# Output stores from another queue, and projections that wait for their operands half by half

## The chip, the cores and the metric

The kernel runs on one core of a Trainium2 chip. The metric is the time of one execution on the device in microseconds; of several runs the median is given. The core has five engines that run on their own and meet at semaphores: TensorE (PE in the profile, PEld for its weight loads), VectorE (DVE), ScalarE (ACT), GpSimd (POOL) and SyncE (SP). DMAs are issued from SP, ACT and POOL. Those of SP and ACT show in the profile as the hardware queues, those of POOL as the software queue.

## What is computed

One inference step of an encoder for 256 prompt tokens and 64 sample tokens (320 in all), model width 1024, two layers. Cut to what matters:

```
for i in range(2):
    up, us = rmsnorm(xp, g_mix[i]), rmsnorm(xs, g_mix[i])
    yp, ys = mlstm(up, us) if i == 0 else pool_mix(up, us)       # layer 0 / layer 1
    xp, xs = xp + yp, xs + ys
    kp, vp = rmsnorm(mem, g_mem[i]) @ w_k, rmsnorm(mem, g_mem[i]) @ w_v
    xp = xp + cross_attend(rmsnorm(xp, g_xattn[i]), kp, vp, w_q, w_o)
    xs = xs + cross_attend(rmsnorm(xs, g_xattn[i]), cache_k[i], cache_v[i], w_q, w_o)
    xp = xp + peer(rmsnorm(xp, g_ffn[i]), w_peer_q, peer_keys, expert_u, expert_v)
    xs = xs + peer(rmsnorm(xs, g_ffn[i]), ...)
y_prompt, y_sample = rmsnorm(xp, g_final), rmsnorm(xs, g_final)  # and all the carried states
```

All is in fp32. The products with the weights are made of three products of rounded halves: of the weight and of the activation a high part (fp32r) and a low part (the rest) are formed, and hi·hi, hi·lo and lo·hi are summed.

## The kernel before

It is written engine by engine by hand: each engine has one program, in which the order of the code is the order of execution, and semaphores hold the engines together. Nothing is scheduled.

**Tiles.** The 320 tokens are three tiles of 128, 128 and 64 rows (`TILES`). To use a normalised tile `u` as an operand, PE turns it: `transposes` (L800) makes two jobs per tile, each of four 128-column blocks, so three tiles give six jobs in the order tile 0 first half, tile 0 second half, tile 1 first half and so on. For each job ACT copies the high part out of PSUM (`copy_transposes`, L1194) and DVE subtracts to get the low part (`empty_transposes`, L1569), and then adds one to `d_emptied`. Job n of the D banks is thus done when `d_emptied` is n + 1. `DJ[stage]` is the number of a stage's first job; the four D banks are used in turn, and `d_bank(n)` makes PE wait until job n − 4 is emptied. The first half of a tile holds the rows k = 0 to 3 of the eight 128-deep slices (k) over which a product with a weight is summed, the second half k = 4 to 7.

**Weights** come by 2 MB chunks from SP (L510). ACT rounds a chunk's quarters (L1232 in the projections, L1366 in the PEER stage), adding to `w_hi_ready`, POOL (in some stages DVE) forms the rest (L467, L700), adding to `w_lo_ready`. Both write a ring that holds four quarters.

**Products** on PE have two forms. `split_block` (L804, matmuls L815 to L817) has the weights stationary and takes a quarter q (two slices k) at a time, 24 matmuls for one block of 128 features; `feature_major` (stages qk and xq) and the PEER query (pq) use it. `token_major` (L831, matmuls L844, L847, L852) has the tokens stationary and goes through k = 0 to 7, for each k over all the tiles, five hi and three lo matmuls of 512 columns where there are three tiles, four and two where there are two; two calls make the 1024 columns. Stages v, o, out, memk, memv and xo use it.

**The stages with the changed waits**, in the order of the program: the first norm's transposes, then qk (once); the mLSTM output's transposes (yT), eight state products (L963), then out (once); and for each of the two layers memT then memk (the memory's keys), xn then the turned memory keys (memkT, L984) then xq, the attention (`av`) then xo, and fn then pq. Before each of those products PE waits once for the whole set of transposed halves, `d_emptied` at the stage's last job. In the attention, `av_order` makes 16 jobs per layer: for each head two transposes of probabilities and two feature jobs (L1019), and DVE writes each feature job out as one slice k of the next product's operand, in four operations (L1815 to L1818). The last head's two features are the jobs 14 and 15.

**The end.** After the last PEER stage DVE finishes `x` (L2072), ACT takes the row statistics (L1180, L1181), DVE normalises the tiles in the order samples, prompt 0, prompt 1 (L1562, adding to `u_ready`), and POOL stores each as it is ready (L761), then waits for all stores (L762 to L765). POOL's work before that is the gathering of expert rows (L729). Line L242, named in the profile for the end of each engine's program, is where the block of the five programs is closed: each engine runs a DRAIN there and they meet at a barrier.

## Time and profile before

| | us |
|---|---|
| median of 3 runs | 2447.32 |
| lowest, highest | 2447.02, 2448.24 |
| the profiled execution's own time | 2450.18 |
| its span, first to last instruction | 2448.4 |
| PE busy | 2360.5 |
| PE's weight loads busy | 2095.0 |
| DVE, ACT, POOL busy | 1496.3, 1280.1, 1458.7 |
| mean granted TensorE clock | 0.988 |

A stretch of work is named by its start in the span. The setup and mLSTM stages are at 0 to 245 us, layer 0's memory, attention and projections at 245 to 400, its PEER stage at 400 to 1330, and the same of layer 1 up to 2430, with the output at the very end. Where idle time of an engine is shown in square brackets, the name behind the arrow is the operation that ended it. Names of engines with a q (POOLq, PEldq) are their instruction queues, for instructions that do no work on data. The share of busy time tells little here, since PE is at 96% nearly throughout; what matters is what PE waits for at a stage's start, and what stands behind the last matmul.

### The profile page before, as it was taken

To read this page: it belongs to the slowest core of one execution; us is meant where nothing else is said; L and a number is where in the kernel's file an instruction comes from. 1 tells how busy PE (TensorE), PEld (TensorE's weight loads), DVE (VectorE), ACT (ScalarE), POOL (GpSimd) and SP (SyncE) were. 2 spreads that over 40 slices of the span, in tenths; PEclk is the share of its full clock that TensorE was granted. 3 is DMA by queue.
4 is the path that set the end of the run, shared out by engine and by line. 5 is a ranking of instruction groups with operands and counts; after the bars stand their busy time and mean duration, and the time that the engine had idled before them with its cause. 6 is when DMAs were issued, how large, how long until landed. Compare 5 with 4: busy or idle time off the path is not lost.

```text
span 2448.4 us, 43649 instructions
## 1 busy us (share of the span) xinstructions
PE 2360.5 (96%) x13862; PEld 2095.0 (86%) x13862; DVE 1496.3 (61%) x3045; ACT 1280.1 (52%) x2864; POOL 1458.7 (60%) x1803
## 2 busy tenths in 40 slices
PE   7999999999999999999999999999999999999997
PEld 7766877998999999888887877998999999888885
DVE  3244444897755332788886444897665332788885
ACT  4334544455765555545454544455775555545453
POOL 6634436689668888773210436688668888773210
PEclk9998999999999999999999999999999999999998
DMA  5324433244788886899986333243688886899983
GB/s 204 130 86 133 160 138 121 104 148 144 230 294 269 272 262 226 318 344 330 358 321 254 138 138 112 97 155 128 226 296 282 259 270 227 313 349 326 358 317 125
DMA packets 219860, 548.60 MB, mean 224 GB/s; under 512 B 49569, under 2 KB 135585, under 8 KB 194414
## 3 DMA queue, kind: packets, MB, share of 16 engines
q1 hardware_dynamic: 135422, 402.62, 47.6%
q0 software_dynamic: 31536, 117.53, 13.0%
q10 hardware_dynamic: 52800, 27.27, 3.9%
q8 instruction: 42, 0.69, 0.1%
q14 instruction: 60, 0.49, 0.1%
HBM read 478.81 MB, written 68.55 MB: 224 GB/s over the span
## 4 chain that ended last, share of the span: by engine, by line
PE 65%; DVE 12%; POOL 12%; issue 8%; ACT 2%; DMA 1%; POOLq 0%; SPq 0%; ACTq 0%; DVEq 0%
PE psum L1046 28%; POOL w_split L700 12%; PE psum L815 7%; PE psum L817 6%; PE psum L816 6%; PE psum L847 6%; PE psum L852 3%; PE psum L1103 2%; DVE arena L1870 1%; DVE arena L1908 1%; PE psum L1068 1%; PE psum L1001 1%; DVE arena L1910 1%; PE psum L1019 1%; DVE arena L1840 1%
## 5 line engine op out<-in xcount | busy, mean ns | idle before, releaser
L700 POOL TENSOR_TENSOR w_split<-w_ring,w_split 128x256 fp32r<-128x256 f32 x1152 | 890.5, 789 | 235.0 <-ACT w_split L1366 179.6
L815 PE MATMUL psum<-uT_split,w_split 128*128 128x320 f32 x2560 | 813.9, 318 | 20.9 <-POOL w_split L700 10.9
L817 PE MATMUL psum<-uT_split,w_split 128*128 128x320 f32 x2560 | 793.8, 310 | 0.0
L816 PE MATMUL psum<-uT_split,w_split 128*128 128x320 f32 x2560 | 793.6, 310 | 0.0
L1366 ACT ACTIVATE w_split<-w_ring 128x256 fp32r<-128x256 f32 x1152 | 473.3, 418 | 465.6 <-PE psum L817 439.4
L815 PEld LDWEIGHTS psum<-uT_split,w_split 128*128 128x128 f32 x2560 | 483.6, 189 | 41.1 <-POOL w_split L700 25.3
L1046 PE MATMUL psum<-v_hl,p_hl 128*128 128x512 f32 x2064 | 483.2, 389 | 1.9 <-DVE p_hl L2021 1.9
L816 PEld LDWEIGHTS psum<-uT_split,w_split 128*128 128x128 f32 x2560 | 484.0, 189 | 0.0
L817 PEld LDWEIGHTS psum<-uT_split,w_split 128*128 128x128 f32 x2560 | 483.1, 189 | 0.0
L1046 PEld LDWEIGHTS psum<-v_hl,p_hl 128*128 128x128 f32 x2064 | 386.8, 188 | 84.9 <-DVE p_hl L2021 3.1
L2015 DVE TENSOR_TENSOR arena<-arena 128x256 f32<-128x256 f32 x256 | 176.8, 728 | 334.5 <-ACT arena L1495 291.5
L467 POOL TENSOR_TENSOR w_split<-w_ring,w_split 128x256 fp32r<-128x256 f32 x328 | 240.2, 748 | 118.8 <-ACT w_split L1232 106.1
L1478 ACT ACTIVATE v_hl<-w_ring 128x1024 fp32r<-128x1024 f32 x172 | 182.3, 1060 | 228.8 <-PE psum L1046 198.6
L1232 ACT ACTIVATE w_split<-w_ring 128x256 fp32r (+1 forms) x416 | 157.8, 413 | 242.6 <-PE psum L852 171.9
L2026 DVE TENSOR_TENSOR v_hl<-w_ring,v_hl 128x1024 fp32r<-128x1024 f32 x172 | 211.6, 1230 | 101.2 <-ACT v_hl L1478 89.9
L1046 PE MATMUL psum<-uT_split 128*128 128x512 f32 x1008 | 242.1, 389 | 0.0
L1046 PEld LDWEIGHTS psum<-uT_split 128*128 128x128 f32 x1008 | 189.2, 188 | 39.3
L735 POOL DMA_INDIRECT cst<-acts,cst x128 | 141.7, 1107 | 39.0 <-issue 39.0
L729 POOL DMA_INDIRECT w_ring<-peer_v,cst x64 | 80.9, 1264 | 115.9 <-DVE psum L1948 102.3
L1478 ACT ACTIVATE uT_split<-w_ring 128x1024 fp32r<-128x1024 f32 x84 | 89.0, 1060 | 111.3 <-PE psum L1046 98.1
L729 POOL DMA_INDIRECT arena<-peer_v,cst x64 | 68.4, 1069 | 114.7 <-DVE psum L1948 106.8
L2026 DVE TENSOR_TENSOR uT_split<-w_ring,uT_split 128x1024 fp32r<-128x1024 f32 x84 | 103.0, 1227 | 46.5 <-ACT uT_split L1478 46.4
(294 smaller groups left out, 2597.8 us busy)
## 6 DMA issues: line engine op xcount, KB each, us to landing
w_ring<-peer_u SPq DMA_DIRECT2D x128, 1024.0 KB, 5.1
w_ring<-peer_v SPq DMA_DIRECT2D x256, 512.0 KB, 5.5
arena<-gates SPq DMA_DIRECT2D x32, 1024.0 KB, 8.1
gates<-w_ring POOLq DMA_DIRECT2D x22, 1024.0 KB, 7.2
weighed<-arena ACTq DMA_DIRECT2D x36, 512.0 KB, 6.7
arena<-weighed SPq DMA_DIRECT2D x36, 512.0 KB, 7.1
w_ring<-w_pq SPq DMA_DIRECT2D x8, 2048.0 KB, 8.1
gates<-arena POOLq DMA_DIRECT2D x10, 1024.0 KB, 8.7
```

The costliest lines, as they stand in the source:

```text
L467: eng.tensor_tensor(dst, raw, chunk_quarter(name, local, i, q, 0)[1].bitcast(F32), ALU.subtract).then_inc(w_lo_ready, 1)
L700: pool.tensor_tensor(split_pair(q, 1), quarter(raw, m, q), split_pair(q, 0).bitcast(F32), ALU.subtract).then_inc(w_lo_ready, 1)
L729: pool.indirect_dma_start(out=row_slot[k % SLOTS], out_offset=None, in_=t_in["peer_v"].rearrange("l b p k d -> (l b p k) d"), in_offset=ba ...
L815: pe.matmul(bank[:, 0:TOK], hi, uT_hi[:, k, :], start=k == 0, stop=False)
L816: pe.matmul(bank[:, 0:TOK], hi, uT_lo[:, k, :], start=False, stop=False)
L817: last = pe.matmul(bank[:, 0:TOK], lo, uT_hi[:, k, :], start=False, stop=k == KD - 1)
L1046: last = pe.matmul(psum[:, 2 + 2 * t + n, :], lhs, vh[:, part, n * 512:(n + 1) * 512], start=False, stop=False, skip_group_check=True)
L1232: act.activation(dst, raw, ACT.Copy).then_inc(w_hi_ready, 1)
L1366: act.activation(split_pair(q, 0), quarter(raw, m, q), ACT.Copy).then_inc(w_hi_ready, 1)
L1478: act.activation(vhl[b % 3][:, 0, :], v_raw[b % 4], ACT.Copy).then_inc(vhi_ready, 1)
L2015: return dve.tensor_tensor(halves_of, halves_of, g_blocks[buffer][:, :, r // 2, :, r % 2], ALU.mult)
L2026: dve.tensor_tensor(vhl[b % 3][:, 1, :], v_raw[b % 4], vhl[b % 3][:, 0, :].bitcast(F32), ALU.subtract).then_inc(v_split, 1)
```

## The change

Two things are changed. The three output stores and the final waits for all stores stand at the end of SP's program and no longer at the end of POOL's. And where PE waited for all jobs of a transposed set, it waits for one more than the first halves' last job but one before the slices k = 0 to 3, that is for the last tile's first half, and for the last tile's second half before k = 4 (before the quarters 0 and 2 of the first block in `split_block`, before every k in `token_major`). Before the attention's output projection it waits at each k for the job that made this feature.

```diff
@@ sync, at its end
+            for place, t in enumerate(ORDER["final"]):
+                off, rows = TILES[t]
+                sp.wait_ge(u_ready, 18 + place + 1)
+                dst = t_out["y_p"][off:off + rows] if t < 2 else t_out["y_s"]
+                sp.dma_start(dst, u[0:rows, t, :]).then_inc(y_stored, 16)
+            sp.wait_ge(mem_stored, 64)
+            sp.wait_ge(pool_stored, 32)
+            sp.wait_ge(state_stored, 64)
+            sp.wait_ge(y_stored, 48)
@@ gpsimd, at its end
-            for place, t in enumerate(ORDER["final"]):
-                off, rows = TILES[t]
-                pool.wait_ge(u_ready, 18 + place + 1)
-                dst = t_out["y_p"][off:off + rows] if t < 2 else t_out["y_s"]
-                pool.dma_start(dst, u[0:rows, t, :]).then_inc(y_stored, 16)
-            pool.wait_ge(y_stored, 48)
-            pool.wait_ge(mem_stored, 64)
-            pool.wait_ge(pool_stored, 32)
-            pool.wait_ge(state_stored, 64)
@@ tensor: split_block
+            def split_block(i, per, base, bank, filled=a_filled, quarters=range(4), turned_tiles=None):
                 for q in quarters:
+                    if turned_tiles is not None and q % 2 == 0:
+                        pe.wait_ge(d_emptied, DJ[turned_tiles] + 5 + q // 2)
                     pe.wait_ge(w_lo_ready, at(i, 4 * per, base + q + 1))
@@ tensor: token_major
+                            parts=(uT_hi, uT_lo), k_ready=None):
                 for k in range(KD):
                     ...
+                    if k_ready is not None:
+                        pe.wait_ge(d_emptied, k_ready(k))
                     pe.wait_ge(w_hi_ready, ready)
@@ tensor: the stages
-            pe.wait_ge(d_emptied, DJ["mixn0"] + 6)
-            feature_major("qk", 4)
+            feature_major("qk", 4, "mixn0")
...
-            pe.wait_ge(d_emptied, DJ["yT"] + 6)
-                token_major("out", "out", c, TILES, base=3 * c)
+                token_major("out", "out", c, TILES, base=3 * c, k_ready=lambda k: DJ["yT"] + 5 + k // 4)
...
-                pe.wait_ge(d_emptied, DJ[f"memT{l}"] + 4)
-                    token_major(f"memk{l}", f"memk{l}", c, mt, base=2 * c, parts=(mT_hi, mT_lo))
+                    token_major(f"memk{l}", f"memk{l}", c, mt, base=2 * c, parts=(mT_hi, mT_lo),
+                                k_ready=lambda k: DJ[f"memT{l}"] + 3 + k // 4)
...
-                pe.wait_ge(d_emptied, DJ[f"xn{l}"] + 6)
-                feature_major(f"xq{l}", 2)
+                feature_major(f"xq{l}", 2, f"xn{l}")
...
-                pe.wait_ge(d_emptied, DJ[f"av{l}"] + 16)
+                features = {2 * h + k - 2: n for n, h, k in av_order(l) if k >= 2}
-                    token_major(f"xo{l}", f"xo{l}", c, TILES, base=3 * c)
+                    token_major(f"xo{l}", f"xo{l}", c, TILES, base=3 * c, k_ready=lambda k: features[k] + 1)
...
-                pe.wait_ge(d_emptied, DJ[f"fn{l}"] + 6)
-                            split_block(i, 8, split_base(l, m), a_bank(AJ[f"pq{l}"] + m, i, 8))
+                            split_block(i, 8, split_base(l, m), a_bank(AJ[f"pq{l}"] + m, i, 8),
+                                        turned_tiles=f"fn{l}" if m == 0 else None)
```

On PE, at the start of layer 0's output projection xo, behind the last feature job (`arena` holds the values, `uT_split` and `p_hl` the attention's features for prompt and samples, `w_split` the split weights). Before:

```order
L847 MATMUL psum<-w_split,uT_split 128x512 [waits d_emptied,w_hi_ready]
L847 MATMUL psum<-w_split,uT_split 128x512
L847 MATMUL psum<-w_split,uT_split 128x512 [waits d_emptied]
L847 MATMUL psum<-w_split,uT_split 128x512
L844 MATMUL psum<-w_split,p_hl 128x512 [waits d_emptied]
L852 MATMUL psum<-w_split,uT_split 128x512 [waits w_lo_ready]
L852 MATMUL psum<-w_split,uT_split 128x512
L852 MATMUL psum<-w_split,p_hl 64x512
L847 MATMUL psum<-w_split,uT_split 128x512 [waits w_hi_ready]
```

And now, with the first row of the next slice as the last:

```order
L854 MATMUL psum<-w_split,uT_split 128x512 [waits d_emptied,w_hi_ready]
L854 MATMUL psum<-w_split,uT_split 128x512
L854 MATMUL psum<-w_split,uT_split 128x512 [waits d_emptied]
L854 MATMUL psum<-w_split,uT_split 128x512
L851 MATMUL psum<-w_split,p_hl 128x512 [waits d_emptied]
L859 MATMUL psum<-w_split,uT_split 128x512 [waits w_lo_ready]
L859 MATMUL psum<-w_split,uT_split 128x512
L859 MATMUL psum<-w_split,p_hl 64x512
L854 MATMUL psum<-w_split,uT_split 128x512 [waits w_hi_ready,d_emptied]
```

No instruction moved. The first wait on `d_emptied` is for another number, the waits of the three banks (one per tile) are as they were, and each later slice has a wait on `d_emptied` beside the one on `w_hi_ready`.

At the end of POOL's program before:

```order
L729 DMA arena<-peer_v,cst 128x1024 [waits rows_used] x4
L761 DMA y_s<-arena 64x1024 [waits u_ready]
L761 DMA y_p<-arena 128x1024 [waits u_ready] x2
L242 UNCONDITIONAL_BRANCH [waits pool_stored,state_stored,mem_stored,y_stored]
```

And at the end of SP's program now, behind the last expert rows that SP loads:

```order
L569 DMA w_ring<-peer_v 128x1024 [waits v_split] x11
L625 DMA y_s<-arena 64x1024 [waits u_ready]
L625 DMA y_p<-arena 128x1024 [waits u_ready] x2
L242 UNCONDITIONAL_BRANCH [waits state_stored,y_stored,pool_stored,mem_stored]
```

The stores and the four waits moved as they are; POOL's program now goes from its last gather to the end of the block.

## Rows read from the trace of the kernel before

**Rows 1.** The page: shares of the chain of work that ended last.

```profile
PE 65%; DVE 12%; POOL 12%; issue 8%; ACT 2%; DMA 1%; POOLq 0%; SPq 0%; ACTq 0%; DVEq 0%
```

**Rows 2.** Line L242: engine, operation, count, ns min/median/max, first to last start (us).

```profile
L242 POOLq EVENT_SEMAPHORE  x2: 17/17/17, 2448.2 to 2448.3; - x2
L242 SPq DRAIN  x1: 123/123/123, 2414.8 to 2414.8; - x1
...
L242 POOLq DRAIN  x1: 9136/9136/9136, 2439.0 to 2439.0; - x1
```

**Rows 3.** Line L2188, the barrier at the kernel's start, same columns.

```profile
L2188 POOLq DRAIN  x1: 183/183/183, 0.3 to 0.3; - x1
```

**Rows 4.** Timeline of the end: start, us, engine, line, operation [idle before <-releaser].

```profile
2356.71 0.94 POOL L729 DMA_INDIRECT arena<-peer_v,cst  x1 [4.56 <-DVE psum L1948]
...
2434.21 1.28 DVE L1562 SCALAR_TENSOR_TENSOR arena<-x_sb,small,gain_rows 128x1024 f32<-128x1024 f32 x1
...
2435.80 0.54 POOL L761 DMA_DIRECT2D y_p<-arena  x1 [0.81 <-DVE arena L1562]
```

**Rows 5.** DMA issues of 2436 to 2449: queue, count, KB each, us to landing.

```profile
y_p<-arena POOLq DMA_DIRECT2D x1, 512.0 KB, 3.0
```

**Rows 6.** DMA issues of 2414 to 2422, same columns.

```profile
w_ring<-peer_v SPq DMA_DIRECT2D x1, 512.0 KB, 3.2
```

**Rows 7.** Timeline of 2411 to 2416: the wait that this SP load follows.

```profile
2413.19 1.23 DVE L2026 TENSOR_TENSOR v_hl<-w_ring,v_hl 128x1024 fp32r<-128x1024 f32 x1 [3.29 <-ACT v_hl L1478]
...
2414.44 0.33 SPq L569 DMA_DIRECT2D w_ring<-peer_v  x1
```

**Rows 8.** Waits of PE's matmuls: us in total, times, longest.

```profile
PE psum L847 <- DVE v_hl L1569: 4.3, 2, 2.5
...
PE psum L815 <- DVE uT_split L1569: 2.8, 2, 1.4
PE psum L847 <- DVE p_hl L1818: 2.5, 2, 1.2
```

**Rows 9.** Timeline of layer 0's memory keys, 247 to 250.

```profile
247.24 2.48 DVE L1569 TENSOR_TENSOR v_hl<-psum,v_hl 128x512 fp32r<-128x512 f32 x4
...
249.78 0.50 PE L847 MATMUL psum<-w_split,v_hl 128*128 128x512 f32 x1 [1.86 <-DVE v_hl L1569]
```

**Rows 10.** Timeline of the attention's end, layer 0, 354 to 362.

```profile
353.82 3.61 PE L1019 MATMUL psum<-arena 128*128 128x256 f32 x22
...
357.09 0.21 DVE L1818 TENSOR_TENSOR p_hl<-psum,p_hl 128x64 fp32r<-128x64 f32 x1
...
358.66 1.19 PE L847 MATMUL psum<-w_split,uT_split 128*128 128x512 f32 x4 [1.24 <-DVE p_hl L1818]
```

**Rows 11.** Timeline of fn and the first query block, layer 0, 395 to 400.

```profile
394.93 3.14 DVE L1569 TENSOR_TENSOR uT_split<-psum,uT_split 128x512 fp32r<-128x512 f32 x6
...
395.75 2.78 POOL L700 TENSOR_TENSOR w_split<-w_ring,w_split 128x256 fp32r<-128x256 f32 x4
...
398.13 0.42 PE L815 MATMUL psum<-uT_split,w_split 128*128 128x320 f32 x1 [1.40 <-DVE uT_split L1569]
```

**Rows 12.** Timeline of the first projection, 14 to 20.

```profile
16.66 0.63 PE L815 MATMUL psum<-uT_split,w_split 128*128 128x320 f32 x1 [1.77 <-POOL w_split L467]
```

**Rows 13.** The last chain before stage out: start us, us, what.

```profile
205.56 7.13 PE psum L963 x16
```

**Rows 14.** Timeline of 275 to 280: the turned memory keys, between xn and xq.

```profile
277.10 2.04 PE L984 MATMUL psum<-cst,arena 128*128 128x128 f32 x16 [0.23 <-DVE uT_split L1569]
```

**Rows 15.** PE's own waiting instructions at L779 (bank waits in the PEER stages).

```profile
L779 PEldq EVENT_SEMAPHORE  x32: 51/51/51, 404.8 to 1571.8; - x32
```

**Rows 16.** PE in xo's first chunk, 358 to 373: busy us, mean ns, idle before.

```profile
L847 PE MATMUL psum<-w_split,uT_split 128*128 128x512 f32 x32 | 8.8, 395 | 1.2 <-DVE p_hl L1818 1.2
...
L847 PEld LDWEIGHTS psum<-w_split,uT_split 128*128 128x128 f32 x32 | 5.9, 188 | 3.0 <-DVE p_hl L1818 1.4
```

**Rows 17.** Busy by stretch: length, PE, PEld, DVE, ACT, POOL, PEclk, DMA share, GB/s.

```profile
399.00:402.40 3.40, 3.40 (x15) 3.40 (x15) 0.00 (x0) 0.83 (x2) 1.47 (x2) 0.50 0.00 0
```

More of the change, by code:

```diff
@@ L805, in u_transposes @@
                 transposes(stage, lambda t, rows, b: u[0:rows, t, b * P:(b + 1) * P], TILES, 3 * norm, u_ready)
-            def split_block(i, per, base, bank, filled=a_filled, quarters=range(4)):
+            def split_block(i, per, base, bank, filled=a_filled, quarters=range(4), turned_tiles=None):
                 for q in quarters:
+                    if turned_tiles is not None and q % 2 == 0:
+                        pe.wait_ge(d_emptied, DJ[turned_tiles] + 5 + q // 2)
                     pe.wait_ge(w_lo_ready, at(i, 4 * per, base + q + 1))
@@ L818, in split_block, with feature_major @@
                     last.then_inc(quarter_used if q < 3 else filled, 1)
-            def feature_major(name, n_chunks):
+            def feature_major(name, n_chunks, turned_tiles):
                 def pair(i):
                     for m in range(8):
-                        split_block(i, 8, SPLIT[name, 0][0] + 4 * m, d_bank(DJ[name] + m, i, 8), d_filled)
+                        split_block(i, 8, SPLIT[name, 0][0] + 4 * m, d_bank(DJ[name] + m, i, 8), d_filled,
+                                    turned_tiles=turned_tiles if m == 0 else None)
                 if n_chunks == 2:
@@ L831, in token_major @@
             def token_major(stage, name, local, tiles, bank_of=d_bank, filled=d_filled, jobs=DJ, base=0, folded=True,
-                            parts=(uT_hi, uT_lo)):
+                            parts=(uT_hi, uT_lo), k_ready=None):
                 banks = [None] * len(tiles)
```

## The prediction, made before the changed kernel ran

> **What bounds the kernel now.** I read the page's shares of the last chain first [rows 1]. PE has 65% of it, and DVE and POOL have 12% each, which they spend in the PEER stages that the change leaves alone. So time can be won only where PE stands idle at the start of a product, or behind the last matmul. For the first I read the waits of PE's matmuls by line [rows 8], and for each place the timeline. The reader should see which operation ended the wait, since that is what a finer wait can pass. For the second I read the timeline of the end and the instructions of line L242, where the profile shows each engine's DRAIN.
>
> **The end.** DVE finishes the last tile at 2434.21 + 1.28 = 2435.49, POOL starts the store 0.31 us later at 2435.80 [rows 4], and the store lands 3.0 us after that, at 2438.8 [rows 5]. No engine has work left, yet the span ends at 2448.4. Between stands one row: a DRAIN on POOL's queue from 2439.0 with 9136 ns, and the barrier's last semaphores at 2448.2 to 2448.3, 17 ns each [rows 2]. The DRAIN begins after POOL has waited for the stores, so it lies wholly on the path. SP's DRAIN took 123 ns, right behind a load that SP had just issued [rows 2].
>
> With the change POOL has nothing left after its last gather at 2356.71 + 0.94 = 2357.65 [rows 4]. If its DRAIN takes the same 9.1 us there, it ends near 2366.8, with 70 us to spare before the last store. The end is then SP's. SP started a load 0.02 us after the DVE operation that it waited for (2413.19 + 1.23 = 2414.42, start 2414.44) [rows 7], and that load, of the same 512 KB and with no other transfer about, took 3.2 us from issue to landing [rows 6]. So the store goes out at 2435.51 and lands at 2438.7. Then I put 0.15 us to the DRAIN (POOL's stood some 0.2 us behind its landing), 0.12 us for SP's DRAIN, and 0.25 us for the barrier (from POOL's end, 2439.0 + 9.14 = 2448.15, to 2448.4) [rows 2]. This makes 2439.2, which is **9.2 us** less. The store itself gains 0.1 us of that, the rest is the DRAIN. The store is a write where the row is a read; a write that took a microsecond more would take that off.
>
> The Trainium skill, page "DMA: Bandwidth & Descriptors", section "Specifications", puts the first byte of a DMA from SP or ACT at about 0.6 us and of one from GpSimd at about 1 us. By that the store would land 0.4 us sooner than by the rows, and the sum would be 0.4 us better. The two rows of equal size show 3.2 us from SP and 3.0 us from POOL from issue to landing, so the trace doesn't bear this out, and I go by the rows.
>
> **The projections**, in the order of the program.
>
> *qk* (once). PE's first matmul at 16.66 was released by POOL's split of the weights, not by the transposes [rows 12]. Nothing is gained.
>
> *out* (once). Between the yT jobs and out stand eight state products, and the bank waits of the last need the yT jobs emptied already. In the chain PE runs through them for 7.13 us and then goes on [rows 13]. Nothing is gained. *xq* (twice) is the same case: the fourth group of turned memory keys needs a bank that is free only when job 6 of xn is emptied, so the wait is before those transposes [rows 14] and not before xq. Nothing.
>
> *memk* (twice). Four half tiles, which DVE empties in 2.48 us, 0.62 us apart (247.24 to 249.72), and PE starts at 249.78 [rows 9]. Rows k = 0 to 3 need the first three. PE starts 0.62 us sooner, and what it finds next is there: the fourth is emptied 0.62 us later, while PE needs over 3 us for four slices. The stage then runs as a ring of PE, ACT and DVE at one pace, so its end moves with its start. 2 x 0.62 = **1.2 us**.
>
> *xo* (twice). PE ends the attention's products at 353.82 + 3.61 = 357.43 and starts xo at 358.66, when DVE has written the last feature [rows 10]. That feature is needed at k = 7 only. What is late next? The bank of the third tile needs job 14 emptied, which is at 357.09 + 0.21 = 357.30 [rows 10], so it is free when PE comes. The two idle times are 2.5 us in sum [rows 8], and all of it goes: **2.5 us**. Slice k = 7 comes some 12 us later and doesn't wait.
>
> *pq* (twice). DVE empties six halves in 3.14 us; the last two, of the 64-row tile, are 0.33 us apart, which is what is left of 3.14 us after four of 0.62 us, halved. PE starts at 398.13, right behind the last, and POOL's first quarter has been split since 395.75 + 0.7 [rows 11]. Quarter 0 needs the fifth half only. Idle 2.8 us in two [rows 8], of which 2 x 0.33 = **0.7 us** goes. Between nothing and the whole 2.8 us I take this, since the fifth half is the last that quarter 0 needs.
>
> *The waits added.* Five single waits go, and eight come in each of ten calls of `token_major`, some 80. Behind each stands all of PE's work, and ACT, which refills the weights' ring when PE has used them. PE's instruction for a further wait takes 51 ns [rows 15]. If each were exposed, this is 80 x 0.051 = 4.1 us. But in xo's first chunk, where slice 0 already carries the waits for three banks beside those for the weights, the 32 matmuls of L847 have 1.2 us of idle before them in all, and that is the wait at the start [rows 16]. So satisfied waits pass while PE works on what is queued, and I take 0, with 4.1 us as the upper bound. Below nothing it can't go, since a wait makes nothing faster.
>
> *The clock.* After a sparse stretch of PE the granted clock stood at 0.50 from 399.0 to 402.4, the lower level of 1.2 GHz [rows 17], in the middle of the first query blocks. Such a stretch costs up to half its length, 1.7 us, and one lies near four of the six starts that move. A start that moves by 0.3 to 1.3 us can lose such a stretch or meet one. I take no change, and up to three either way, 5 us, as the outer bound.
>
> **The sum.** 9.2 + 1.2 + 2.5 + 0.7 = 13.6 us. The stages behind hang on these by semaphores and carry their transfers along, so a start that is earlier stays so. The profiled execution took 2450.18 us with a span of 2448.4, and would take 2436.6. The median of the runs shown is 2447.32, so I predict 2447.32 - 13.6 = **2433.7 us**.
>
> **The rivals.**
> *The DRAIN is longer under the profiler.* The profiled execution is 2.9 us over the median. If all of that is in the DRAIN, the true one takes 6.3 us and the gain is 2.9 us less: 2436.6 us. Nothing else in the profile speaks for it.
> *The last 9 us stay.* The DRAIN might be long because it comes at the very end, whoever waits there, or POOL's might wait for the others. Then the change doesn't do what it says at the end and only the projections' 4.4 us are left: 2442.9 us. For this speaks that at the kernel's start POOL's took 183 ns [rows 3], so its length is no constant. Against it: the DRAINs of the other engines end before, and SP's took 0.12 us in the midst of its load [rows 2].
> The Trainium skill, page "VectorE: DVE Perf Modes", section "The DRAIN you can't avoid", has the DRAINs at a program's start and end at about 12 ns, the same on all five engines. By that rule there is no long DRAIN to hide and this rival would be the forecast, 2442.9 us; the row of 9136 ns speaks against the rule here.
> *The waits are exposed.* 4.1 us at 51 ns each: 2437.8 us.
> *Slower.* A wait at each k could keep PE from loading the next weights ahead. Then each of the 80 costs a weight load of 188 ns [rows 16] and its own 51 ns, 19.1 us together, and the time is 2433.7 + 19.1 = 2452.8 us. It decides from 0.23 us a wait, (13.6 + 4.9) / 80. Against it stands that the weights' waits at each k of today don't do this [rows 16].
> *The starts don't pay*, because a transfer or another engine is late next by as much: 2447.32 - 9.2 = 2438.1 us. Against it: SP issues each of these loads when a chunk two before has been used, so they move with the stages.
>
> **How the numbers follow.** The forecast 0.75; the profiler's share 0.07; the last 9 us stay 0.05; waits exposed 0.05; starts don't pay 0.04; slower 0.02; something else that is faster 0.02. A measurement of this kernel can tell some 0.2% (4.9 us) from no change: faster is below 2442.4, slower above 2452.2. Faster sums to 0.93, the same 0.05, slower 0.02. The range takes in the exposed waits and the starts that don't pay, and for the clock two stretches less on the lower side: 2430.3 to 2438.3.
>
> **What would show it.** In the changed kernel's trace POOL's DRAIN should stand near 2357 to 2367 less the few us of the projections, with 9 us, and the span should end under 0.6 us behind the last landing. PE's idle before L847 of xo should be gone, that before memk 0.6 us shorter and before pq 0.3 us shorter; before qk, out and xq nothing should change. The slices k = 1 to 7 should stand as close as now. The prediction is wrong if POOL's DRAIN moves with the end, if SP's store takes well over 3.2 us, or if idle time of PE grows inside the chunks.

## The result, and the profile of the changed kernel

The changed kernel took 2438.02 us in the median of four executions (2437.41 to 2443.15). The kernel before, timed beside it, took 2447.78 us in the median of four (2447.02 to 2455.87). The ratio is 0.9955 with a 95% interval of 0.9944 to 0.9967. So the change makes the kernel faster, by 9.8 us by the medians and by about 11 us (8 to 14) by the ratio. 13.6 us were forecast, and 2433.7 us as the time. The range of 2430.3 to 2438.3 us holds it, near its upper end.

The profiled execution took 2443.15 us with a span of 2441.3 us, the longest of the four. Its span is 7.1 us shorter than that of before, 2448.4 us. So two things are to be found: what the change won, and what kept 3 to 4 us in the executions together, and 6.5 us in this profile, from being won.

The shares of the last chain, from the page. The row answers to [rows 1].

```profile
PE 63%; POOL 13%; DVE 12%; issue 9%; ACT 2%; DMA 1%; POOLq 0%; SPq 0%; ACTq 0%; DVEq 0%
```

**The end.** The instructions of line L242 (engine, operation, count, ns min/median/max, first to last start), beside [rows 2]:

```profile
L242 POOLq DRAIN  x1: 11644/11644/11644, 2359.1 to 2359.1; - x1
...
L242 SPq COMPARE_BRANCH  x1: 41/41/41, 2440.9 to 2440.9; - x1
L242 SPq DRAIN  x1: 7/7/7, 2441.1 to 2441.1; - x1
L242 SPq EVENT_SEMAPHORE  x1: 17/17/17, 2441.3 to 2441.3; - x1
```

The timeline of the end (start, us, engine, line, operation), beside [rows 4]:

```profile
2436.79 1.74 SPq L625 DMA_DIRECT2D y_p<-arena  x2
2436.88 1.29 DVE L1566 SCALAR_TENSOR_TENSOR arena<-x_sb,small,gain_rows 128x1024 f32<-128x1024 f32 x1
```

The two stores of y_p among the DMA issues (KB each, us from issue to landing), beside [rows 5]:

```profile
y_p<-arena SPq DMA_DIRECT2D x2, 512.0 KB, 2.7
```

POOL's DRAIN now starts at 2359.1, and POOL takes up its last gather 0.2 us later:

```profile
2359.30 0.94 POOL L739 DMA_INDIRECT arena<-peer_v,cst  x1 [4.49 <-DVE psum L1952]
```

The DRAIN takes 11.6 us and ends near 2371, 67 us before the last store. DVE ends its last operation at 2436.88 + 1.29 = 2438.17, the store lands 2.7 us after its issue, and SP's DRAIN takes 7 ns. From the end of DVE's last operation to the end of the span it is 3.1 us. Before it was 2448.4 - 2435.49 = 12.9 us [rows 2, 4]. The end gained 9.8 us, of which 9.2 were forecast.

**The starts.** The first is the timeline of layer 0's memory keys, beside [rows 9].

```profile
247.59 2.48 DVE L1573 TENSOR_TENSOR v_hl<-psum,v_hl 128x512 fp32r<-128x512 f32 x4
...
249.54 0.73 PE L854 MATMUL psum<-w_split,v_hl 128*128 128x512 f32 x2 [1.26 <-DVE v_hl L1573]
```

The next is the timeline of the attention's end in layer 0, beside [rows 10].

```profile
351.74 5.45 PE L1023 MATMUL psum<-arena 128*128 128x256 f32 x32
...
357.00 1.17 PE L854 MATMUL psum<-w_split,uT_split 128*128 128x512 f32 x4
...
358.15 0.21 DVE L1822 TENSOR_TENSOR p_hl<-psum,p_hl 128x64 fp32r<-128x64 f32 x1
```

PE begins the memory keys 0.53 us before DVE has written the fourth half (247.59 + 2.48 = 250.07). It runs from the attention's products into xo with no idle time, 1.36 us before the last feature is written at 358.36. The waits of PE that [rows 8] showed have gone the same way: the 4.3 us before L847 behind v_hl are 2.7 us before L854 now, and the row of 2.5 us behind p_hl has no successor.

```profile
PE psum L854 <- DVE v_hl L1573: 2.7, 2, 1.4
```

**Where the time came back.** DVE does the same operations in the same order in both kernels, so each can be compared with itself. The changed kernel's profile is 0.34 us late at the memory tiles, and 0.2 us of that stand already at 11.5 us, before PE's first product. It is 0.25 us early behind layer 0's memory keys, 1.68 us early behind xo and 1.98 us early behind the first query block, as the steps have it. Then it falls back: by 1.5 us at 590, in a stage that the change leaves alone, and by 3.7 us between 731 and 763. It is 3.3 us late from there on. In layer 1 it wins nothing at memk, where 0.62 us were forecast. It wins 1.46 us at xo, loses 0.74 us at the query blocks, and wins 1.5 us at 1696, where the kernel before has a half-clock stretch of its own. Between 1720 and 2200 it loses 1.5 us more, with no half-clock stretch there, and DVE's last operation ends 2.67 us later than before. At most of these places the granted clock differs. The columns are: stretch, length, PE, PEld, DVE, ACT and POOL busy, PEclk, DMA share, GB/s. First the changed kernel:

```profile
201.40:218.40 17.00, 15.69 (x45) 11.92 (x46) 11.82 (x23) 8.01 (x18) 3.78 (x6) 0.50 0.18 58
389.10:399.30 10.20, 7.74 (x35) 7.25 (x36) 7.55 (x14) 6.70 (x17) 3.82 (x6) 0.50 0.58 229
590.50:593.90 3.40, 3.40 (x15) 3.40 (x14) 3.30 (x9) 0.83 (x2) 1.16 (x2) 0.50 0.65 272
733.90:737.30 3.40, 3.40 (x15) 3.40 (x14) 2.37 (x4) 0.83 (x2) 2.84 (x4) 0.50 0.46 188
1351.70:1358.50 6.80, 5.39 (x14) 4.12 (x15) 3.69 (x7) 1.32 (x3) 3.86 (x6) 0.50 0.38 154
1498.50:1508.70 10.20, 8.49 (x36) 7.92 (x37) 5.25 (x11) 4.47 (x12) 5.21 (x6) 0.50 0.17 71
```

And the kernel before at two of the places:

```profile
590.50:593.90 3.40, 2.86 (x20) 2.63 (x21) 3.27 (x12) 0.42 (x1) 0.29 (x1) 1.00 0.66 205
733.90:737.30 3.40, 3.40 (x26) 3.40 (x25) 3.25 (x4) 1.92 (x5) 3.40 (x5) 1.00 0.33 135
```

The six stretches of the changed kernel at 0.50 (1.2 GHz) sum to 51.0 us; two of 3.4 us more, near 123 and 143, stand in both kernels alike. Before, the trace has seven of them from 201 on: 17 us from 201, and 3.4 us each at 392, 399, 1351, 1495, 1502 and 1696, together 37.4 us. That is 13.6 us more at the lower level. If PE sets the pace all through it, this costs half, 6.8 us, and 6.5 us are missing. That the two agree proves little: of what is missing, the 1.5 us behind 1720, the 0.3 us ahead of the change and 1.7 us of idle time at 731 (below) are not the clock's. At 590 the row shows the price by itself: PE is busy all the time, with 15 matmuls where the row of before at 733.9, as long and at the full level, has 26. What PE did ahead of it is the same in both kernels. The timeline of the changed kernel:

```profile
588.85 0.55 PE L1086 MATMUL psum<-cst,shared 128*128 128x128 f32 x3 [1.72 <-DVE shared L1973]
```

And of the kernel before:

```profile
590.83 0.55 PE L1082 MATMUL psum<-cst,shared 128*128 128x128 f32 x3 [1.72 <-DVE shared L1969]
```

PE idles for 1.72 us in front of the slot transposes and then works without a gap. Once the clock falls 1.7 us later, and once, with the work 2 us further on, it stays up.

At 731 there is more than the clock. The timeline of PE in the changed kernel:

```profile
733.00 0.41 PE L819 MATMUL psum<-uT_split,w_split 128*128 128x320 f32 x1 [2.22 <-POOL w_split L710]
```

The same matmul in the kernel before:

```profile
731.76 0.41 PE L815 MATMUL psum<-uT_split,w_split 128*128 128x320 f32 x1 [0.52 <-POOL w_split L700]
```

PE stands idle for 1.7 us more there, behind a split of the weights that came later (POOL idles 3.67 us for it, and 1.97 us before). The clock falls at 733.9, behind this idle time.

### The profile page after: what moved, and what is told of

Same layout as the page of the kernel before. It is cut to its first block, busy times and chain, and to the rows that moved or that the text cites. A ratio compares the mean times of both kernels' runs of the same rounds, so it can differ in the third digit from the quotient of the medians.

```text
span 2441.3 us, 43727 instructions
## 1 busy us (share of the span) xinstructions
PE 2363.6 (97%) x13862; PEld 2097.5 (86%) x13862; DVE 1497.8 (61%) x3045; ACT 1279.5 (52%) x2864; POOL 1449.9 (59%) x1800
## 3 DMA queue, kind: packets, MB, share of 16 engines
q0 software_dynamic: 31168, 116.22, 12.9%
## 4 chain that ended last, share of the span: by engine, by line
PE 63%; POOL 13%; DVE 12%; issue 9%; ACT 2%; DMA 1%; POOLq 0%; SPq 0%; ACTq 0%; DVEq 0%
PE psum L1050 28%; POOL w_split L710 12%; PE psum L819 7%; PE psum L821 6%; PE psum L820 6%; PE psum L854 5%; PE psum L859 3%; PE psum L1107 2%; DVE arena L1874 1%; DVE arena L1912 1%; PE psum L1072 1%; PE psum L1005 1%; DVE arena L1914 1%; PE psum L1023 1%; DVE arena L1844 1%
```

## The experiments

The executions of one kernel scatter more than the prediction allowed for. So each kernel below was timed several times beside runs of the kernel before on the same chip. The three groups of runs used three chips, and their medians of before were 2449.73 us (24 runs), 2450.8 us (11) and 2451.12 us (9); the last run had its own, 2451.43 us (11).

| kernel | median, us (lowest to highest) | ratio to before, 95% interval |
|---|---|---|
| the change again | 2440.71 (2436.58 to 2445.49) | 0.9956 (0.9940 to 0.9972) |
| stores on SP alone | 2440.05 (2437.99 to 2442.24) | 0.9951 (0.9934 to 0.9968) |
| finer waits alone | 2448.27 (2445.39 to 2451.38) | 0.9989 (0.9979 to 0.9999) |
| stores on POOL, final waits on SP | 2446.49 (2443.37 to 2454.75) | 0.9983 (0.9971 to 0.9995) |
| the change, PE kept busy | 2429.22 (2427.38 to 2430.98) | 0.9907 (0.9893 to 0.9922) |
| stores alone, PE kept busy | 2432.38 (2429.28 to 2433.52) | 0.9918 (0.9905 to 0.9931) |
| the change, each added wait five times | 2438.40 (2436.55 to 2447.33) | 0.9950 (0.9934 to 0.9966) |
| stores, and xo's waits alone | 2439.83 (2437.08 to 2447.64) | 0.9958 (0.9944 to 0.9972) |
| the change, PE kept busy at more gaps | 2427.85 (2426.71 to 2429.90) | 0.9905 (0.9890 to 0.9921) |
| the change, PE kept busy at fn alone | 2437.93 (2435.05 to 2442.84) | 0.9941 (0.9928 to 0.9955) |
| the change, PE kept busy at yT alone | 2434.47 (2432.59 to 2436.99) | 0.9934 (0.9920 to 0.9947) |
| the change, pq's wait written first | 2439.78 (2436.91 to 2445.29) | 0.9954 (0.9938 to 0.9970) |

**The changed kernel again**, with no edit.

> The changed kernel once more, profiled and timed. In its first profile the end gained 9.7 us (12.9 us behind the last DVE operation before, 3.2 us after), but the work ahead of it took 7 us more than the prediction's sum has it. Theory 'chance of the body': of that, 5.3 us stood at two places that the change does not touch (a stretch at half clock from 590.5, 1.5 us, and late loads with another such stretch from 731, 3.8 us). Then this profile shows nothing lost at least at one of the two places, its span is 2436 to 2439 us, and the median is 2437 to 2438 us. Rival 'the change costs it': both places lose the same again, and the span is 2441 us.

Its windows at the two places (columns as above):

```profile
588.20:591.60 3.40, 3.40 (x15) 3.40 (x14) 3.30 (x8) 0.83 (x2) 0.99 (x2) 0.51 0.65 270
731.60:735.00 3.40, 3.40 (x15) 3.40 (x14) 1.97 (x4) 0.83 (x3) 2.67 (x4) 0.50 0.58 241
```

Both places lose again: 1.5 us at the first, 3.1 us at the second. The span is 2440.8 us and the median 2440.71 us. "Chance of the body" fell in the form I gave it. The losses come back at the same work. The rival, that the change costs them, held in this run. They are not the only ones: this profile loses 3.0 us more between 1720 and 1900, where it has a half-clock stretch of its own, at 1861.

**The stores alone.** POOL's block of three stores and four final waits moves to SP as in the change. PE's waits stay those of before.

> The kernel before with its output stores and final waits on SyncE, PE's waits as they were. Theory 'the end is the whole gain': 9.7 us less than before by the profile's end, some 2437.6 us, and nothing is left for the projections. Rival 'the DRAIN is longer under the profiler': 6.3 to 6.8 us less, 2440.8 us, and the rest of the measured 10 us comes from the projections. By the prediction's own step: 9.2 us less, 2438.2 us.

The DRAIN on POOL, as it stands in this kernel:

```profile
L242 POOLq DRAIN  x1: 10972/10972/10972, 2358.2 to 2358.2; - x1
```

The median is 9.7 us below that of before, by the ratio 12 us (8 to 16). The medians agree with the profile's 9.8 us, and the ratio is no smaller. The rival that the DRAIN is long only under the profiler would leave 6.3 to 6.8 us, and it is off. So this kernel is as fast as the changed one: the seven executions of the change and the five of this one, on one chip, differ by 0.6 us in the mean, the change being the slower, with an interval of 3.2 us either way.

The profile of this kernel has no half-clock stretch at 588 or 731. But it has one at layer 0's memory keys, where the kernel before has none, and one of 10.2 us at the first query blocks, where the kernel before has twice 3.4:

```profile
249.10:255.90 6.80, 5.89 (x14) 4.64 (x15) 1.61 (x4) 0.98 (x3) 0.00 (x0) 0.50 0.40 169
395.90:406.10 10.20, 8.72 (x39) 7.72 (x38) 5.46 (x11) 4.91 (x13) 4.79 (x7) 0.50 0.37 151
```

From 201 on its stretches sum to 47.6 us, with PE's program as before. So a profile can have 10 us more at half clock than the one of before without the finer waits, and how much of the changed kernel's 13.6 us is their doing isn't shown.

**The finer waits alone.** The stores and final waits are back on POOL:

```diff
-                sp.dma_start(dst, u[0:rows, t, :]).then_inc(y_stored, 16)
+                pool.dma_start(dst, u[0:rows, t, :]).then_inc(y_stored, 16)
```

> The changed kernel with its output stores and final waits back on GpSimd: PE's finer waits alone. By the prediction's steps: 4.4 us less than before, 2443.0 us. Theory 'the starts are won and the clock takes them': in the profile memk gains 0.6 us, xo 1.2 us, pq 0.3 us in each layer, but more half-clock time about the first query blocks and the memory keys, and 0 to 2 us less in all, 2445.4 to 2447.4 us. Rival 'the waits are exposed': the idle time inside the chunks grows by up to 4 us, same total.

They give 1.5 us by the medians and 2.7 us by the ratio (0.2 to 5.1), about the upper end of the clock theory's 0 to 2 us. The interval takes in the 4.4 us of the steps too, so the time doesn't decide between them. Its profile has the half-clock stretches at both places:

```profile
587.70:591.10 3.40, 3.40 (x14) 3.40 (x14) 3.30 (x8) 0.83 (x2) 1.05 (x2) 0.50 0.65 265
731.10:734.50 3.40, 3.40 (x15) 3.40 (x14) 2.42 (x5) 0.83 (x2) 2.82 (x4) 0.50 0.41 170
```

**Stores on POOL, final waits on SP.**

```diff
+                pool.dma_start(dst, u[0:rows, t, :]).then_inc(y_stored, 16)
...
+            sp.wait_ge(y_stored, 48)
```

> The changed kernel with the three output stores back on GpSimd's queue, and only the final waits on SyncE. GpSimd's DRAIN then starts when the last store is issued, not when it has landed. Theory 'the DRAIN has a length of its own, some 9 us': it starts some 0.6 us behind the last issue, 2.5 us sooner than before, so the end gains 2.5 us and the projections' part: 2 to 3 us over what the finer waits alone give, and some 7 us more than the changed kernel. Rival 'the DRAIN waits for what its queue has in flight and then 9 us': no gain at the end, the same time as with all on GpSimd.

```profile
core 0 of [0], span 2442.1 us
...
L242 POOLq DRAIN  x1: 9709/9709/9709, 2432.2 to 2432.2; - x1
```

DVE's last operation ends at 2431.90 here. The DRAIN starts 0.3 us later, while POOL is still issuing the last store:

```profile
2432.21 0.54 POOL L766 DMA_DIRECT2D y_p<-arena  x1 [0.80 <-DVE arena L1566]
```

It ends at 2441.9, which is 9.1 us behind the end of that issue at 2432.75, and 9.1 us is what it took with nothing left to do. The stores have landed by 2435.3, when SP passes its last wait. From DVE's end to the span's end it is 10.2 us, 2.7 us less than with the waits on POOL too. The medians differ by 1.8 us. So the DRAIN has a length of its own, and it runs whether or not it is last. The rival, in which it waits for its queue and then takes its 9 us, fell. In this kernel the finer waits are those of the change, and yet 731 shows no stretch at half clock:

```profile
587.50:590.90 3.40, 3.40 (x15) 3.40 (x14) 3.18 (x10) 0.84 (x2) 1.25 (x2) 0.50 0.67 267
731.00:734.40 3.40, 3.40 (x26) 3.40 (x25) 3.38 (x5) 1.20 (x4) 2.92 (x4) 1.00 0.24 96
```

From 201 on this profile has 37.4 us at half clock, as much as that of before, and its last DVE operation ends 3.6 us earlier: with the same half-clock time most of the 4.4 us are there. The kernel with the finer waits alone has 40.8 us and the loss at 731, and ends its last DVE operation only 0.3 us earlier.

So the loss at 588 stands in all four profiles with the finer waits so far, and the one at 731 in three of them. Neither stands in the two without them.

**PE kept busy in its gaps.** If the clock takes the gain, then holding the clock must give it back, whichever waits are used. Both kernels get transposes of the identity matrix into a bank that the next real product overwrites:

```diff
+            def keep_busy(bank, n):
+                for _ in range(n):
+                    pe.transpose(bank[:, 0:P], ident, ident)
...
+                    if t == 0 and stage in FILL:      # FILL = {"fn0": 27, "fn1": 27, "memT1": 14}
+                        keep_busy(d_bank(n), FILL[stage])
...
+                keep_busy(d_bank(n), (14, 19, 6)[t])      # before the wait for y_ready
...
+                keep_busy(d_bank(DJ[f"memk{l}"]), 8)      # 12 in the sister
...
+                keep_busy(a_bank(AJ[f"pq{l}"], 0, 8), 8)  # 10 in the sister
...
+                        keep_busy(bank, 12)               # before the wait for picked_ready
```

> The changed kernel with further transposes of the identity matrix (results overwritten) on TensorE in the gaps in which it waits for a norm: 27 before fn, 8 before the first query block, 8 before the memory keys, 14 before layer 1's memory tiles, 12 before the slot transposes, 39 about yT. Theory 'the clock takes back what the starts win': the half-clock stretches from 201, 389, 588, 1349 and 1496 us go, 41 us in all in the changed kernel's first profile, and the time falls by 8 to 20 us; and this kernel is 3 to 5 us faster than its sister with the waits of before. Rival 'the starts win little for another reason': both busy kernels fall alike and lie within 1.5 us of each other. Rival 'these transposes only delay': slower than the changed kernel by up to 10 us.

> The kernel with the stores on SyncE and PE's waits of before, with the same further transposes (10 and 12 in place of 8 where the gaps are wider). Theory 'the clock': 8 to 20 us less than without them, and 3 to 5 us more than its sister with the finer waits, as the prediction's sum has it (4.4 us). Rival 'another reason': within 1.5 us of the sister.

The windows of the first of the two:

```profile
201.00:218.00 17.00, 15.83 (x92) 12.59 (x91) 12.03 (x25) 10.41 (x25) 6.43 (x10) 1.00 0.32 98
390.00:393.40 3.40, 3.40 (x17) 3.28 (x17) 2.03 (x6) 0.59 (x2) 2.12 (x4) 0.50 0.46 159
...
583.00:592.00 9.00, 7.42 (x51) 7.14 (x51) 6.19 (x18) 3.00 (x9) 4.98 (x7) 1.00 0.35 117
1343.00:1352.00 9.00, 8.76 (x41) 6.95 (x42) 4.92 (x12) 3.28 (x10) 3.66 (x6) 1.00 0.35 117
1488.00:1496.00 8.00, 6.46 (x47) 6.08 (x48) 4.02 (x9) 4.24 (x11) 4.92 (x7) 1.00 0.06 22
```

The long stretch from 201 is at the full level, and so are the slot transposes, the memory keys and layer 1's fn. The time falls to 2429.22 us: by the ratios 12 us below the changed kernel, and 8 us below the stores alone for its sister, the second kernel, which has PE's waits of before. That this much hangs on the gaps, and comes back with the clock, is shown. The finer waits are now worth 3.2 us by the medians, 2.7 us by the ratios, and 3.2 us between the two profiles (2427.7 and 2430.9 us of span). This is at the edge of the 3 to 5 us expected and above the rival's 1.5 us, but the nine executions leave it anywhere from 0.3 to 5.2 us.

The two profiles say more. This is the same DVE operation of layer 1's PEER stage in the first and in the second:

```profile
1705.22 0.69 DVE L2017 TENSOR_TENSOR arena<-psum,shared 128x1024 f16<-128x1024 f16 x1 [17.52 <-PE psum L830]
```

```profile
1709.60 0.69 DVE L2013 TENSOR_TENSOR arena<-psum,shared 128x1024 f16<-128x1024 f16 x1 [17.52 <-PE psum L826]
```

Behind all six starts the finer waits lead by 4.4 us, the sum of the prediction. (Each kernel has one half-clock stretch at its query blocks, the first at 390, the second at 1492.6.) The lead falls to 3.2 us at 1880, and in between stands a stretch that the second doesn't have:

```profile
1847.50:1850.90 3.40, 3.40 (x15) 3.40 (x14) 1.72 (x2) 0.83 (x2) 3.04 (x4) 0.50 0.90 225
```

The second kernel still has its waits for xo, which the other has lost:

```profile
PE psum L856 <- DVE p_hl L1832: 2.5, 2, 1.2
```

**Five waits for one.**

```diff
-                        pe.wait_ge(d_emptied, k_ready(k))
+                        for _ in range(5):
+                            pe.wait_ge(d_emptied, k_ready(k))
```

> The changed kernel with each of its 80 added waits in the token-major products issued five times, 320 waits more, all satisfied. Theory 'satisfied waits pass while PE works': the same time as the changed kernel, within 2 us. Rival 'exposed': 320 x 0.051 = 16 us more. Rival 'they keep PE from loading weights ahead': no more than that again, since the first of five would already do it.

PE in xo's first chunk, 355 to 371 (columns as in [rows 16]):

```profile
L855 PE MATMUL psum<-w_split,uT_split 128*128 128x512 f32 x30 | 8.3, 395 | 0.0
L855 PEld LDWEIGHTS psum<-w_split,uT_split 128*128 128x128 f32 x31 | 5.8, 188 | 1.6
```

The 320 further waits are in the program, packed by two: the trace has 230 waiting instructions of 51 ns at these lines, where the changed kernel has 70. If each were exposed, the 160 more would cost 8.2 us, and not the 16 us of the expectation. The median is 2438.40 us, 0.9950 of before where the change has 0.9955 and 0.9956. The matmuls of the chunk have no idle time in front of them. Satisfied waits cost nothing that shows here while PE has matmuls to work on. The 8.2 us of exposed waits are excluded too.

**The stores, and xo's waits alone.** Of PE's edits only the row-by-row waits in xo are made.

> The kernel with the stores on SyncE and, of PE's finer waits, only the row-by-row waits of the attention's output projection. By the prediction's step 2.5 us less than the stores alone (some 2437.5 us beside 2440), with 1.2 us in each layer to be seen in the profile. Theory 'the clock gives or takes': the two starts are won, but the difference of the medians lies anywhere from -5 to +2 us, by which half-clock stretches the execution meets.

The median is 2439.83 us, the ratio 0.9958 where the stores alone have 0.9951. In the profile xo starts 1.4 us earlier in both layers, as in the changed kernel. In the time the 2.5 us are not to be seen: the intervals of the two ratios overlap almost wholly. This run does not tell the clock from any other loss. It only shows that a gain of this size drowns when PE's gaps are left to the clock.

**Where the clock matters.** Two kernels have the extra transposes in one place each, and one has them in two more places (17 in front of the o projection's second bank, 11 in the first head of the mixing).

> The changed kernel with the further transposes at the fn stages alone (27 before the norm's first tile, 8 before the first query block, in both layers), that is beside the changed starts of pq. Theory 'the clock at the changed starts takes the gain': the 10.2 us half-clock stretches about 390 and 1496 us go and give 3 to 6 us, nearly all that the finer waits had lost. Rival 'it is lost elsewhere': under 2 us.

> The changed kernel with the further transposes at the yT stage alone, where the clock fell for 13.7 to 17.1 us in the kernel before too. Theory: this part of the busy kernel's gain has nothing to do with the change and is 3 to 5 us; with the fn part alone beside it the two sum to the busy kernel's 10 us less 1 to 3 us for the memory keys and the slot transposes. Rival 'DVE and ACT set the pace there': under 1 us.

> The busy kernel with the finer waits, and further transposes of the identity at two more gaps: 17 in front of the second bank of the o projection's second chunk (TensorE idles 2.3 us there and then ran at half clock from 144.2 us) and 11 in the first head of the mixing (1.5 us idle). Theory 'the clock': the stretch from 144 us goes, 1 to 2 us less than the busy kernel, some 2427.5 us. Rival: nothing of that stretch was on the path, same as the busy kernel within 1 us.

At fn alone the ratio falls from 0.9955 to 0.9941, 3.4 us; by the two intervals this isn't clear of noise. In its profile the two stretches of 10.2 us are 3.4 us each:

```profile
396.30:399.70 3.40, 3.40 (x16) 3.28 (x17) 2.17 (x6) 0.73 (x2) 2.26 (x4) 0.50 0.50 154
1502.20:1505.60 3.40, 3.40 (x16) 3.40 (x16) 1.76 (x6) 0.38 (x1) 0.18 (x1) 0.50 0.02 5
```

At yT alone it falls to 0.9934, 5.1 us, just clear of noise. The long stretch from 201 stands in the kernel before, too, so this could probably be won there as well, which no run tried. The two sum to 8.5 us, and the whole set gives 12 us. In the third kernel the stretch near 144 us is gone:

```profile
144.00:148.00 4.00, 3.21 (x14) 2.04 (x12) 1.89 (x3) 3.97 (x11) 0.05 (x1) 1.00 0.24 102
```

Three of 3.4 us are left behind it, at 389, 1488 and 1846. It is 1.4 us faster by the medians, and 0.0002 by the ratios, which were taken on two chips. It is the fastest kernel of the study at 2427.85 us, 0.9905 of before, but that it beats its forerunner isn't certain.

**The wait of pq, written first.** In the changed kernel pq gained less than the 0.33 us forecast: it starts 0.25 us behind the fifth half, where before it started 0.05 us behind the sixth. One wait was moved ahead:

```diff
                 u_transposes(f"fn{l}", norm)
+                pe.wait_ge(d_emptied, DJ[f"fn{l}"] + 5)
                 pe.wait_ge(keys_loaded, 16 * (l + 1))
```

> The changed kernel with the wait of the first query block for the fifth half written ahead of the other waits of that block, not behind them. In the changed kernel's traces two waiting instructions of 51 ns stood between the release and the first weight load (starts 0.1 us apart), and the block started 0.25 us behind the fifth half, where the block of before started 0.05 us behind the sixth. Theory 'a wait in its own instruction is paid at the release': the block now starts 0.05 us behind the fifth half, 0.2 us sooner in each layer. Rival 'something else holds it': 0.25 us as before. In the time neither can be told: 2437 to 2441 us.

The changed kernel (its second profile): DVE's six halves, PE's first matmul, and PE's own waiting instructions at L814, the line of the new wait:

```profile
392.46 3.14 DVE L1573 TENSOR_TENSOR uT_split<-psum,uT_split 128x512 fp32r<-128x512 f32 x6
...
395.53 0.38 PE L819 MATMUL psum<-uT_split,w_split 128*128 128x320 f32 x1 [1.26 <-POOL w_split L710]
```

```profile
L814 PEldq EVENT_SEMAPHORE  x4: 51/51/51, 15.9 to 1501.3; - x4
```

With the wait first:

```profile
392.96 3.14 DVE L1574 TENSOR_TENSOR uT_split<-psum,uT_split 128x512 fp32r<-128x512 f32 x6
...
395.83 0.63 PE L819 MATMUL psum<-uT_split,w_split 128*128 128x320 f32 x1 [0.84 <-DVE uT_split L1574]
```

From the start of the six halves to the matmul it is 3.07 us in the one and 2.87 us in the other, 0.2 us sooner, and the same in layer 1. The releaser is now the half itself. The wait that is written first is carried by the weight load. The others become instructions of their own, which PE has still to pass after the release. In this kernel only two are left at L814, those of qk. The time doesn't tell the two kernels apart.

## Why the prediction was right, and where it was not

*The end* was right. The store goes out, the DRAIN is hidden, and SP takes its place with 7 ns. The forecast was 9.2 us and 9.8 us came, mostly since the store took 2.7 us to land and not 3.2. The 3.2 us were those of a load on SP; compared store with store, SP's landed 0.3 us sooner than POOL's 3.0, and not later, as I took it. The medians of the stores alone confirm the gain, 9.7 us.

On the DRAIN the Trainium skill (page "VectorE: DVE Perf Modes", section "The DRAIN you can't avoid") has some 12 ns on every engine at a program's end. By this rule only the projections' 4.4 us would have been won. The rows at the end show 9.1 to 12.2 us on POOL in every profile, and on PE, DVE and ACT 4.27, 1.32 and 0.32 us, which end before the last store lands. SP has 7 ns where it stores last, and 123 ns where it doesn't. So the rule fits SP at the end of the changed kernel, and no other engine.

*memk, xo and pq.* In the changed kernel's profile layer 0 gained 0.59, 1.43 and 0.30 us, where 0.62, 1.24 and 0.33 were forecast; xo of layer 1 gained 1.46 us. In layer 1 memk gained nothing and pq lost 0.74 us, in half-clock stretches of 6.8 and 10.2 us where before had 3.4 and twice 3.4. The 0.30 us of pq come with a caution, since PE's start itself moved only by 0.13 us against DVE's halves. The term took the release for the start and left out the 0.2 us of waiting instructions behind it. That is the one place seen where the waits added were not free. Whether qk, out and xq gained anything no run isolated.

*The waits added* were free in the midst of the matmuls, as taken: the fivefold waits cost nothing that the executions can tell.

*The clock* is the step that failed: "I take no change, and up to three either way, 5 us, as the outer bound." The mechanism stood in the text, but I gave it no sign and no part in the sum. I also put such stretches near four of the six starts, where the trace of before has them near three (memk of layer 1 and both pq), and I left out the long one at 201. The profile shows 13.6 us more at half clock, worth up to 6.8 us, and 6.5 us are missing; some 3.5 us of these aren't the clock's. With PE kept busy the profiles have the 4.4 us in full behind the six starts and 3.2 us at the end, and the executions 2.7 to 3.2 us. Without it the finer waits are worth 2.7 us by one comparison (0.2 to 5.1), and nothing measurable by the other, the change beside the stores alone (0.9955 and 0.9956 beside 0.9951). So the starts were moved as forecast, and of their 4.4 us between nothing and 3 us were left at the end. That the clock takes the rest is what the profiles show at single places; the executions are too few to show it by the time.

*The level.* 2447.32 us was the median of three runs that lay close together. The runs of the kernel before made later went from 2446.74 to 2459.27 us. A time of before that is too low by some us makes the forecast time too low by as much. The gain, not the time, is what the sum could foretell. That the first median lies in the range is in part luck: the second of the same kernel, 2440.71 us, lies above it.

*The rivals.* The measured 2438.02 us is, by the number, that of "the starts don't pay" (2438.1) and of "the waits are exposed" (2437.8). Neither mechanism was at work at the starts: they moved, nothing else was late there, and five times the waits cost nothing. But what the rival says of the whole, that the projections' 4.4 us don't reach the end, is close to what the executions show. A time that fits a rival does not make its reason true.

*What stays open.* The half-clock stretch near 590 stands in all six profiles that have all the finer waits and no extra transposes, and in none of the three without them or with xo's alone. Of the four that have the finer waits and extra transposes only the one with those at fn alone has it. That the work comes sooner isn't the reason by itself: with xo's waits alone it comes 1.7 us sooner than before, and the stretch isn't there. Why the clock falls, with the same idle time before it, no run settles. Nor is the loss at 731 explained: it stands in three of the same six, and in a fourth, with five waits for one, one of 1.5 us stands at 755. I call it neither chance nor the change's doing.

## What to carry to other kernels

Look behind the last store: a DRAIN on a queue that has done its work long ago is free, and the same DRAIN on the queue that stores last was 9 us here. Waits on a semaphore that is satisfied cost nothing measurable in the midst of matmuls. The wait that is released last is best written first, so that the weight load carries it: 0.2 us at each of two starts here. Where PE idles for some us before a dense part, count the half-clock time of the trace before counting a start that is a microsecond sooner. Transposes of no use in those gaps gave 12 us here, as much as the whole change.

## What the hardware did that I had not expected

POOL's DRAIN has no one length: 9.14 us with its queue at rest, 9.71 us when it starts on the last store's issue, and 10.97 to 12.17 us when it starts on the last gather's. Two stores on their way added nothing, since it ended 9.14 us behind the end of POOL's issue as well. Behind the gathers it ended 4.5 us after the last gather had landed, in each of the ten profiles that have the landing (the gather took 6.3 to 7.5 us to land). Why it waits for the one and not for the other no run shows. SP's took 7 ns once its stores had landed.

One and the same kernel spreads over up to 9 to 12 us from execution to execution (the changed kernel 8.9 us in seven, the kernel before 12.5 us in 24). The kernels with the yT gaps filled spread over 3.2 to 4.4 us in four or five executions each. Whether the clock makes the whole scatter isn't shown, since only one execution of each kernel has a trace.
